# Attention over compressed and selected keys: the transposes of a unit, and what follows them, one unit later on every engine

## The reference, cut to what matters

```
o_cmp = einsum(p_cmp, v_cmp)                  # 31 compressed keys
o_slc = softmax(q k_slc^T / 8 + bias) v_slc   # 8 blocks of 64 keys, 8 of 8 chosen: all keys
o_win = softmax(q k_win^T / 8 + bias) v_win   # window of 512: all keys
o = g[:, :, 0] * o_cmp + g[:, :, 1] * o_slc + g[:, :, 2] * o_win
y = sigmoid(g_conv) * conv_out + sigmoid(g_attn) * nsa_out
return y @ w_out
```

## Time and profile before

| | |
|---|---|
| time, median of 3 runs | 2091.6 us (2088.53 to 2096.59) |
| span of the profiled execution | 2088.0 us |
| TensorE busy in the span | 1928.5 us, 92% |
| VectorE, ScalarE, GpSimd busy | 755.1, 610.2, 662.6 us |
| the stage of the change | from 1347 to 1502 us of the span |
| TensorE busy in the stage | 137.60 of 155.00 us |
| granted TensorE clock in the stage | 1.00 |

### The profile page before, as it was taken

How to read it: one execution, slowest core, us unless ns; L and a number is a source line. 1 busy time by engine, 2 the same in 40 slices (tenths; PEclk the granted TensorE clock), 3 DMA queues, 4 the chain that set the end, 5 groups by cost and what they waited for, 6 DMA issues and landing times.

```text
span 2088.0 us, 22204 instructions
## 1 busy us (share of the span) xinstructions
PE 1928.5 (92%) x8760; PEld 1253.8 (60%) x8760; DVE 755.1 (36%) x1542; ACT 610.2 (29%) x1102; POOL 662.6 (32%) x384
## 2 busy tenths in 40 slices
PE   5999989589898889989999999989899899999998
PEld 3544337434333333358888878744588578888887
DVE  5551265623222222262899103466421220000002
ACT  3113462111110110052223135366433432222213
POOL 0011333311110110054443133455444324555542
PEclk9999899789999999999999898999999999999999
DMA  9452001779999999953233231111133122232231
GB/s 388 162 237 81 0 1 66 296 308 410 428 427 428 427 428 428 428 207 112 81 105 97 69 102 63 51 32 31 62 108 115 41 91 81 81 121 81 84 118 61
DMA packets 89478, 361.97 MB, mean 173 GB/s; under 512 B 5883, under 2 KB 34939, under 8 KB 74796
## 3 DMA queue, kind: packets, MB, share of 16 engines
q1 hardware_dynamic: 86672, 351.75, 43.3%
q0 software_dynamic: 2304, 8.39, 1.0%
q10 hardware_dynamic: 412, 0.59, 0.1%
HBM read 355.41 MB, written 5.31 MB: 173 GB/s over the span
## 4 chain that ended last, share of the span: by engine, by line
PE 74%; DMA 14%; DVE 5%; ACT 3%; issue 2%; POOL 1%; SPq 0%; POOLq 0%; DVEq 0%; ACTq 0%
PE bank L736 14%; PE bank L738 14%; PE bank L737 14%; DMA slots<-in_w_expert_up 12%; PE bank L711 11%; PE bank L1077 7%; PE bank L1287 2%; PE bank L1307 2%; PE bank L867 1%; PE bank L1102 1%; POOL low_r L2660 1%; PE bank L1276 1%; PE bank L1048 1%; ACT area L1851 1%; DMA slots<-in_w_ada 1%
## 5 line engine op out<-in xcount | busy, mean ns | idle before, releaser
L2660 POOL TENSOR_TENSOR low_r<-slots,high_r 128x2048 fp32r<-128x2048 f32 x86 | 397.2, 4621 | 573.3 <-ACT high_r L1522 573.2
L737 PE MATMUL bank<-xl_r,high_r 128*128 128x512 f32 (+1 forms) x864 | 330.1, 382 | 0.0
L736 PE MATMUL bank<-area_r,high_r 128*128 128x512 f32 x800 | 313.6, 392 | 1.2 <-POOL low_r L2660 1.2
L738 PE MATMUL bank<-area_r,low_r 128*128 128x512 f32 x800 | 312.0, 390 | 0.0
L1522 ACT ACTIVATE high_r<-slots 128x2048 fp32r<-128x2048 f32 x86 | 164.5, 1915 | 413.7 <-PE bank L738 401.8
L1077 PE MATMUL bank<-slots,area 128*64 128x512 f32 x992 | 227.1, 602 | 29.5 <-DMA slots<-in_w_expert_gate 22.0
L737 PEld LDWEIGHTS bank<-xl_r,high_r 128*128 128x128 f32 x864 | 162.9, 189 | 31.6 <-issue 0.5
L1077 PEld LDWEIGHTS bank<-slots,area 128*64 128x64 f32 x992 | 67.3, 137 | 173.1 <-issue 124.7
L736 PEld LDWEIGHTS bank<-area_r,high_r 128*128 128x128 f32 x800 | 150.7, 188 | 33.0 <-POOL low_r L2660 1.4
L738 PEld LDWEIGHTS bank<-area_r,low_r 128*128 128x128 f32 x800 | 150.6, 188 | 31.6
L2473 DVE SCALAR_TENSOR_TENSOR bank<-area,cols,bank 128x512 f32<-128x512 f32 x232 | 153.5, 750 | 0.0
(11 more groups left out here) (417 smaller groups left out, 2890.1 us busy)
## 6 DMA issues: line engine op xcount, KB each, us to landing
slots<-in_w_expert_up SPq DMA_DIRECT2D x32, 2048.0 KB, 16.4
slots<-in_w_expert_down SPq DMA_DIRECT2D x32, 2048.0 KB, 17.2
slots<-in_w_expert_gate SPq DMA_DIRECT2D x30, 2048.0 KB, 15.1
slots<-in_w_in SPq DMA_DIRECT2D x15, 2048.0 KB, 7.9
slots<-in_w_ada SPq DMA_DIRECT2D x11, 2048.0 KB, 13.7
slots<-in_ffn_in_w SPq DMA_DIRECT2D x22, 1024.0 KB, 7.2
slots<-in_ffn_out_w SPq DMA_DIRECT2D x5, 2048.0 KB, 7.8
slots<-in_w_out SPq DMA_DIRECT2D x4, 2048.0 KB, 8.0
```

The costliest lines, as they stand in the source:

```text
L736: nc.tensor.matmul(out, xh, yh, start=start and n == 0, stop=False)
L737: nc.tensor.matmul(out, xh, yl, start=False, stop=False)
L738: last = nc.tensor.matmul(out, xl, yh, start=False, stop=stop and n == len(pairs) - 1)
L2660: nc.gpsimd.tensor_tensor(low_half(m), raw_half(m), high_half(m), ALU.subtract).then_inc(s["w_low"], 1)
```

## The change

Three loops are edited. In iteration v TensorE now does T(v-2) in place of T(v-1), and O one iteration later (v % 4 = 3, from v = 7 on). VectorE does K'(v-3) in place of K'(v-2) and keeps outputs at u % 8 = 5. ScalarE does K(v-3) in place of K(v-2) and splits outputs at u % 8 = 7. S, D, E, R and N stay in their iterations. No instruction is added or taken away, no buffer, bank or semaphore changes, and no transfer is moved.

```diff
@@ TensorE
             for u in range(4 * NH):
                 if u + 2 < 4 * NH:
                     nsa_scores(u + 2)
-                if u:
-                    nsa_transposes(u - 1)
-                if u >= 6 and u % 4 == 2:
+                if u >= 2:
+                    nsa_transposes(u - 2)
+                if u >= 7 and u % 4 == 3:
                     nsa_outputs(u // 4 - 1)
+            nsa_transposes(4 * NH - 2)
             nsa_transposes(4 * NH - 1)
             nsa_outputs(NH - 1)
@@ ScalarE
-                if u >= 2:
-                    nsa_keep_t(u - 2)
-                if u >= 8 and u % 8 == 6:
+                if u >= 3:
+                    nsa_keep_t(u - 3)
+                if u >= 8 and u % 8 == 7:
                     split_mixed(u // 8 - 1)
+            nsa_keep_t(4 * NH - 3)
             nsa_keep_t(4 * NH - 2)
             nsa_keep_t(4 * NH - 1)
@@ VectorE
                 if u >= 1:
                     nsa_inverse(u - 1)
-                if u >= 8 and u % 8 == 4:
+                if u >= 8 and u % 8 == 5:
                     nsa_keep_outputs(u // 8 - 1)
-                if u >= 2:
-                    nsa_keep_t(u - 2)
+                if u >= 3:
+                    nsa_keep_t(u - 3)
             nsa_inverse(4 * NH - 1)
+            nsa_keep_t(4 * NH - 3)
             nsa_keep_t(4 * NH - 2)
             nsa_keep_t(4 * NH - 1)
```

## The result

The changed kernel took 2110.0 us (median of 4 runs, 2108.17 to 2112.37), beside 2094.1 us for the kernel before on the same chip (4 runs, 2088.53 to 2097.21). The ratio, which is taken from the single runs (the two medians alone give 1.0076), is 1.0087, with a 95% interval of 1.0064 to 1.011: slower, by more than was forecast, and 1 us beyond the upper end of the range.

A forecast was written before the change was run, and what follows sets the result against it. TensorE, 92% busy, was taken to be held by waits for ScalarE and VectorE; 0.43 + 0.13 + 0.20 = 0.76 us per block, times 15, adds 11.4 to 2091.6: 2103.0 us, range 2096 to 2109.

The forecast's parts named there:

- What bounds the kernel: TensorE stands still 0.93 us per block; an order of waits on ScalarE and VectorE, not GpSimd, sets the period.
- The change part by part: Slides the block's schedule: GpSimd's extra iteration is worth nothing, and each block gets 0.76 us longer.
- 0.43 for S3 in the place of S1: On TensorE, T3 starts 0.43 us later per block because S3 stands where S1 stood.
- 0.13 for D3: D3's step on VectorE is longer than D2's, so E3 begins another 0.13 us later per block.
- 0.20 for E3: On ScalarE, E3's two steps take 0.20 us more than E2's, ahead of copy K0.
- Idle ahead of S1: Expected sign in the changed profile: TensorE idle 0.8 us ahead of S1 in each block.
- so the clock should hold: TensorE's clock stays at 1.00 at 83% busy, since it read 1.00 at 79% at the stage's start; no cost.
- the rule weighed: Skill's rule: throttled by default, transposes count differently; more idle time in the half-transpose stage could drop TensorE's clock.
- a sign of being wrong: The forecast is wrong if TensorE's clock in the stage is below 1.00.
- the clock falls: Rival, chance 0.03: half clock in 3 blocks of the stage adds 24 us, giving 2127 us.
- in the order of before: After the last counted T1, only two transposes and a product remain, order unchanged; all 15 blocks priced at 0.76 us.
- two waits add up: Rival, chance 0.09: waits ahead of T0 and S1 no longer hidden, or E3 late; 16 to 20 us slower, 2107 to 2112.

The follow-up runs named there:

- Experiment 4: The change, with ScalarE's copy K(u-3) ahead of its exponentials E(u): 2094.1 us, ratio 1.0017 to the kernel before.
- 5: The kernel before, with ScalarE's copy K(u-2) ahead of its exponentials E(u): 2090.9 us, ratio 0.9988 to the kernel before.
- 2: The kernel before with output products, kept outputs and split one iteration later, transposes where they were: 2105.3 us, ratio 1.0074.
- 3: The change with unused matmuls added, i = 0 scores computed twice and scores in the last two iterations: 2102.2 us, ratio 1.0058 to the kernel before.
- 1: The kernel before with transposes and their copies one unit later, outputs where they were: 2083.9 us, ratio 0.9965.
- 6: As 1, with the kept outputs and their split some iterations later: 2082.8 us, ratio 0.9955 to the kernel before.
- 7: The change with more unused matmuls: i = 0 scores three times, its transposes twice, one i = 1 score twice: 2100.8 us, ratio 1.0045 to the kernel before.
- 10: The change with the extra matmuls of 7, but only from unit 8 on: 2103.6 us, ratio 1.0061 to the kernel before.
- 11: As 6, with ScalarE's copy K(u-3) ahead of its exponentials: 2079.9 us, ratio 0.9943 to the kernel before.
- the filled ones: 3, 7 and 10: the change with extra matmuls whose results are not used, ratios 1.0058, 1.0045 and 1.0061 to the kernel before.

## Why the prediction was right and wrong

**What bounds the kernel, right.** TensorE's idle pieces are ended by ScalarE and VectorE, as was argued against the earlier trace rows. Experiment 4 shows it by taking K from behind E, and 5 by uncovering GpSimd where the earlier trace rows has it.

**The change part by part, right.** The three terms, 0.43 for S3 in the place of S1, 0.13 for D3 and 0.20 for E3, came out within 0.02 us on each engine, and the blocks are 9.86 and 10.86 for 9.85 and 10.85. The stage with the clock kept is 11.6 us longer, for 11.4. Idle ahead of S1 is 0.57 and not 0.8: T0's own wait, 0.58 for 0.5, starts it later, and S1 itself starts where it should.

**The step that failed: "so the clock should hold", under the heading of the rule weighed.** It put the clock's cost at nothing, from one stretch of 17 us in which TensorE was busy 79% and the clock 1.00. The profile has 0.97 over the stage, which the prediction itself named as a sign of being wrong, and the clock costs 4.6 us there, beside 11.5 for the waits. Over 10 us the runs show 0.83 at 84% busy, and 1.00 at 62% in another execution of the same program. Busy share of a short stretch doesn't tell the granted clock. What the profiles, one for each run, do show is that it fell in the stage in all three of the change, in 2, 3 and 4, and in none of the kernel before, of 1, 5, 6, 7, 10 or 11. The six that fell have TensorE busy 82 to 88% of the stage, the seven others 88 to 95%. That is an ordering and no rule: 4 and the kernel before have the same 88%, and only 4 fell. By the Trainium skill ("TensorE: Matmul & The Clock Gate", Part 1), the throttled state is the default and activity is what releases it; the trace agrees, in that the clock stayed at 1.00 in both profiles with more matmuls and transposes of no use, 7 and 10. That the transposes count differently (Part 4) no run here tells apart.

**The rival "the clock falls" was mis-sized.** It had 3 whole blocks at half clock, 24 us. The dips are shorter and cost 1.75 to 4.7 us in all. With 2 to 5 us and a chance of one in three instead of 0.03, the range would have reached over 2110.

**The base moved too.** The time is 7.0 us above the forecast of 2103.0. The forecast stood on 2091.6 us, the median of three runs; a fourth run of the same kernel makes it 2094.1. These 2.5 us have nothing to do with the change, and without them the same clock would have left the time inside the range. The other 4.5 are near the 4.6 of the clock in the stage; with executions of one kernel 4 to 17 us apart, that they come so close is in part luck.

**What was not looked at: the last two iterations.** They have no scores, so with the transposes later TensorE stands still 1.01 and 1.76 us ahead of the last product with compressed keys. The iterations at the end were taken to be "in the order of before" and priced at the steady 0.76. Their waits cost no more than that in sum; the half clock behind them cost 2.9 us in two profiles of three. That the idle time there caused the fall is argued, not shown: the third profile has the same idle times and 1.00. The kernel before has a wait of 1.42 us at the same place and 1.00, and 4 fell there with no wait above 0.52 us in the 6 us ahead. The row of the kernel before:

```profile
1493.03 0.63 PE L1287 MATMUL bank<-k,area 128*128 128x128 f32 x4 [1.42 <-ACT slots L1837]
```

**The rival "two waits add up" gave 2107 to 2112, and the time lies in it,** but it was not the cause: the waits ahead of T0 and S1 stayed under the one for K0. A time that fits a rival does not prove it.

**What stays open.** Why the clock falls at one place in one execution and at another in the next, no run here tells, and a reason outside TensorE's idle time is not excluded. Outside the stage the profiles vary from 1921.8 to 1929.8 us. And in run times the clock's share is seen but not fixed: 14 to 18 us over the kernel before for the change, 9 to 13 for the filled ones, with intervals that overlap. The dips were measured in profiles alone.

## What to carry to other kernels

Write a loop of waits as a schedule from the starts in the trace, with the unit index on each item, and slide it: an iteration more of distance is worth nothing if the item queued ahead of the awaited copy moves along with it. Then ask behind which item the one long product stands. Behind T0 it covered the worst wait (6 us gained), behind T1 with the transposes late it left it bare (11.6 us lost). And where a change adds idle time to TensorE, give a fall of its clock a term of its own, of a few microseconds with a fair chance, and look at the loop's last iterations, where work is already missing.

## What the runs showed of the hardware

The granted clock can fall for a few microseconds in a stage in which TensorE is 83% busy and, in the steady part, idle for about 0.6 us at a time at most. The same program had its dips at 1470 to 1480 and 1506 to 1513 in two profiles, and at 1425 to 1450 in a third. Where it fell to 0.53 and 0.55, products of 1.07 and 2.37 us took 1.97 and 3.9. Adding matmuls into the idle pieces (162.8 and 165.5 us busy in the stage for 146.1) left the blocks at 9.86 and 10.86 us, and the clock read 1.00 in the stage in both profiles. Behind the stage, the same product took 3.70 us in one profile and 5.36 in another, behind idle pieces that are the same to 0.01 us. And TensorE's busy time of the same matmuls differs with the order of waits alone: 141.09 and 144.94 us in the stage, both at 1.00.
